# The adaLN condition of a hybrid layer: scale and shift summed on VectorE from the unsplit weights, the first norm applied by feature to the turned x, the gate's weights later in the plan

## What is computed

```
mod = silu(c) @ w_ada + b_ada                  # c: 1024 numbers, w_ada: 1024 x 3072
shift, scale, gate = split(mod, 3)             # 1024 numbers each
h = rms_norm(x, norm_g) * (1 + scale) + shift  # x: 256 x 1024
proj = h @ w_in                                # the four branches' q, k, v, z
...                                            # branches d, c, b, a, merged with sigmoid gates
x = x + gate * (merged @ w_out)
```

## Time and profile before

| | us |
|---|---|
| median of 3 runs | 1190.98 (1190.47 to 1192.14) |
| the profiled execution, its own time | 1190.06 |
| its span | 1188.8 |
| TensorE busy (matmul) | 1153.0 |
| VectorE, ScalarE, GpSimd busy | 735.2, 595.9, 48.3 |
| TensorE's clock granted, mean | 0.989 |

### The profile page before, as it was taken

One profiled execution on the slowest core, in us unless ns is written; L12 is line 12 of the kernel. 1 busy time (PEld: TensorE's weight loads), 2 busy tenths in 40 slices (PEclk: granted clock), 3 DMA queues, 4 the chain that ended last, 5 costly groups with the idle time before them and its releaser, 6 DMA issues.

```text
span 1188.8 us, 16723 instructions
## 1 busy us (share of the span) xinstructions
PE 1153.0 (97%) x7018; PEld 1024.4 (86%) x7018; DVE 735.2 (62%) x936; ACT 595.9 (50%) x824; POOL 48.3 (4%) x80
## 2 busy tenths in 40 slices
PE   6999999999999998999999999999899999999997
PEld 4799888788889987898999988787888989999985
DVE  5944766566677997755556655455767546555643
ACT  5545764344455662654545444445574555443431
POOL 3020100000000000000100000000003000000000
PEclk9999999899999999999999999999899999999999
DMA  9874543265546403543645545554326534546450
GB/s 352 300 246 117 184 137 130 89 230 183 206 146 212 161 1 107 177 141 107 166 159 200 188 164 193 189 187 155 101 93 196 178 106 163 180 172 207 137 188 36
DMA packets 105932, 195.70 MB, mean 165 GB/s; under 512 B 6033, under 2 KB 22561, under 8 KB 105856
## 3 DMA queue, kind: packets, MB, share of 16 engines
q1 hardware_dynamic: 102976, 186.46, 46.5%
q0 software_dynamic: 2880, 8.17, 2.4%
HBM read 193.56 MB, written 1.05 MB: 164 GB/s over the span
## 4 chain that ended last, share of the span: by engine, by line
PE 77%; DVE 12%; ACT 6%; issue 2%; DMA 1%; POOL 1%; SPq 0%; DVEq 0%; ACTq 0%; POOLq 0%
PE product L541 70%; DVE conv_out L2321 4%; ACT w_high L488 3%; DVE w_low L497 3%; DMA w_raw<-in_w_ada 1%; PE small L659 1%; PE small L1795 1%; PE small L1178 1%; ACT drows L2674 1%; PE small L574 1%; PE small L1189 1%; DVE drows L2750 1%; DVE stats L2752 1%; PE small L1816 1%; DVE drows L2765 0%
## 5 line engine op out<-in xcount | busy, mean ns | idle before, releaser
L497 DVE TENSOR_TENSOR w_low<-w_raw,w_high 128x2048 fp32r<-128x2048 f32 (+3 forms) x184 | 404.6, 2204 | 268.3 <-ACT w_high L488 264.5
L488 ACT ACTIVATE w_high<-w_raw 128x2048 fp32r<-128x2048 f32 (+3 forms) x184 | 338.0, 1841 | 180.3 <-PE product L541 161.9
L541 PE MATMUL product<-H_low,w_high 128*128 128x256 f32 x1080 | 307.6, 285 | 2.3 <-DVE w_low L497 1.3
L541 PE MATMUL product<-H_high,w_low 128*128 128x256 f32 x1080 | 305.9, 283 | 0.0
L541 PE MATMUL product<-H_high,w_high 128*128 128x256 f32 x1080 | 305.6, 283 | 0.0
L541 PEld LDWEIGHTS product<-H_low,w_high 128*128 128x128 f32 x1080 | 207.2, 192 | 4.5 <-issue 2.3
L541 PEld LDWEIGHTS product<-H_high,w_low 128*128 128x128 f32 x1080 | 207.2, 192 | 0.3
L541 PEld LDWEIGHTS product<-H_high,w_high 128*128 128x128 f32 x1080 | 207.2, 192 | 0.0
L541 PE MATMUL product<-w_high,H_low 128*128 128x512 f32 (+2 forms) x384 | 150.9, 393 | 0.0
L541 PE MATMUL product<-w_low,H_high 128*128 128x512 f32 (+2 forms) x384 | 149.0, 388 | 0.0
L541 PE MATMUL product<-w_high,H_high 128*128 128x512 f32 (+2 forms) x384 | 148.6, 387 | 0.0
(11 more groups left out here) (370 smaller groups left out, 1528.5 us busy)
## 6 DMA issues: line engine op xcount, KB each, us to landing
w_raw<-in_ffn_w_gate SPq DMA_DIRECT2D x20, 1024.0 KB, 5.1
w_raw<-in_ffn_w_up SPq DMA_DIRECT2D x20, 1024.0 KB, 5.2
w_raw<-in_ffn_w_down SPq DMA_DIRECT2D x20, 1024.0 KB, 5.1
w_raw<-in_w_merge SPq DMA_DIRECT2D x16, 1024.0 KB, 5.0
w_raw<-in_w_ada SPq DMA_DIRECT2D x12, 1024.0 KB, 6.5
w_raw<-in_w_in SPq DMA_DIRECT2D x8, 1024.0 KB, 5.2
w_raw<-in_mem_w_k SPq DMA_DIRECT2D x8, 1024.0 KB, 5.1
w_raw<-in_conv_w_pw SPq DMA_DIRECT2D x16, 512.0 KB, 4.4
```

Of the source, the lines that this page charges most:

```text
L488: k.act.eng.activation(chunk_view(k, k.w_high[j], i), chunk_view(k, k.w_raw[i % k.N_RAW], i), ACT.Copy).then_inc(*k.act.tells("weights_hig ...
L497: k.vec.eng.tensor_tensor(low, raw, high.bitcast(F32), ALU.subtract).then_inc(*k.vec.tells("weights_low", ("weights low", i)))
L541: mm = pe.eng.matmul(bank[:, off:off + wide], a, r, start=b not in started, stop=True, skip_group_check=True)
```

## The change

The weights of scale, shift and gate are no longer split and multiplied on TensorE. `vec_modulation` adds them up on VectorE from the raw buffer, a partition at a time: four operations of 128x512 per chunk, each weight row times its number of silu(c). What is left, a sum over the 128 partitions, is done on TensorE: for scale and shift by 4 matmuls per half with one column of ones (`pe_columns_of`), which puts feature by partition; for the gate by two matmuls with 128x128 ones (`mem()`), which spreads it over all partitions. x is turned first, only scaled by its root, and the norm is applied by feature by ScalarE (`act_first_half`), with low part on VectorE (`vec_first_low`). The plan moves the gate's four chunks between those of `w_in`, and the second half of shift behind the first chunk of `w_in`. x comes on SyncE's queue behind the first two chunks, and `norm_g` as 8 rows of 128.

```
+    first_in, shift = chunks(w_in, KT, [(W_D_Q, 512)]), modulation(ada, "shift", 1)
+    plan.extend(modulation(ada, "scale", 0) + modulation(ada, "shift", 0) + modulation(ada, "scale", 1) + first_in[:1] + shift + first_in[1:])
+    gate = modulation(ada, "gate", 0) + modulation(ada, "gate", 1)
+    for block in ((W_D_V, 512), (W_C_Q, 512), (W_C_V, 512)):
+        plan.append(gate.pop(0))
+        add(w_in, [block])
+    plan.append(gate.pop(0))
...
+def vec_split(k, n):
...
+        if i + 1 < len(k.plan) and k.plan[i + 1][2] and k.plan[i + 1][2][0] == "gate":
+            vec_modulation(k, *k.plan[i + 1][2])
+
+def vec_modulation(k, name, n, first):
+    V, i = k.vec, k.whole_weights[name, n, first]
+    raw, total = chunk_view(k, k.w_raw[i % k.N_RAW], i), k.sums_of[name][:, n * CN:(n + 1) * CN]
+    V.wait_ge("c silu", ("weights", i), "gate bias" if name == "gate" else None)
+    for j in range(CK):
+        number = k.c_silu[:, first + j:first + j + 1]
+        V.wait_ge(V.last)
+        if first + j == 0 and name != "gate":
+            V.eng.tensor_scalar(total, raw[:, j, :], number, None, ALU.mult).then_inc(*V.tells("modulations"))
+        else:
+            V.eng.scalar_tensor_tensor(total, raw[:, j, :], number, total, ALU.mult, ALU.add).then_inc(
+                *V.tells("modulations", (name, n), ("weights low", i)))
...
 def pe_condition(k):
...
+    tr(k.small.take("condition")[:, 0:3 * KT], k.cond_rows[:, :], k.ident[0:3 * KT, 0:3 * KT]).then_inc(*pe.tells("turned", "condition turned"))
+    pe_columns_of(k, "scale", 0)
+    pe_columns_of(k, "shift", 0)
+    for n in range(2):
+        pe_turn_x(k, n)
+    pe_columns_of(k, "scale", 1)
...
+def act_first_half(k, n):
+    A, columns = k.act, k.stat(("columns", n), 2 * CK)
+    for b in range(2):
+        for j in range(2):
+            f = 2 * b + j
+            A.wait_ge(("x turned", n, b), ("columns copied", n), ("whole free", n))
+            A.eng.activation(k.whole[:, f, :], k.small.of(("x", n, b))[:, S * j:S * (j + 1)], ACT.Identity, scale=columns[:, f:f + 1],
+                             bias=columns[:, CK + f:CK + f + 1]).then_inc(*A.tells("whole", k.small.free(("x", n, b))))
+        at = slice(CK * n + 2 * b, CK * n + 2 * b + 2)
+        A.wait_ge(A.last)
+        A.eng.activation(k.H_first.high[:, at, :], k.whole[:, 2 * b:2 * b + 2, :], ACT.Copy).then_inc(*A.tells("operand_high", ("first high", n, b)))
...
 def vec_condition(k):
     V = k.vec
+    V.mark(("whole free", 0))
+    for name in ("scale", "shift"):
+        for first in range(0, KT, CK):
+            vec_modulation(k, name, 0, first)
+    V.wait_ge("condition turned")
+    V.eng.tensor_copy(k.cond_cols[:, :], k.small.of("condition")[:, 0:3 * KT]).then_inc(*V.tells("cond_cols", k.small.free("condition")))
+    vec_modulation(k, "scale", 1, 0)
+    vec_first_columns(k, 0)
+    vec_modulation(k, "scale", 1, CK)
+    vec_first_low(k, 0)
     vec_split(k, 0)
+    for first in range(0, KT, CK):
+        vec_modulation(k, "shift", 1, first)
+    vec_first_columns(k, 1)
+    vec_first_low(k, 1)
     vec_split(k, 1)
...
 def pe_branches(k):
-        yield from pe_block(k, "d_qk", k.H_first, KT, FEATURES)
+        yield from pe_block(k, "d_qk", k.H_first, KT, FEATURES, inside={(0, 28): lambda: pe_columns_of(k, "shift", 1)})
...
     def mem():
+        for n in range(D // CN):
+            bank = k.small.take(("gate sums", n))
+            k.pe.wait_ge(("gate", n), k.small.before(("gate sums", n)))
+            k.pe.eng.matmul(bank[:, :], k.ones, k.gate[:, n * CN:(n + 1) * CN], start=True, stop=True).then_inc(*k.pe.tells("spread", ("gate sums", n)))
+        yield
```

More of the change, by code:

```diff
@@ L731, in vec_add @@
     add.then_inc(*V.tells("x_sums", ("x", norm.name, n, t), k.product.free(bank)))
-MODS = [("scale", 0), ("shift", 0), ("scale", 1), ("shift", 1), ("gate", 0), ("gate", 1)]
+ROWS = {"norm_g": 0, "shift": KT, "scale": 2 * KT}
 def pool_condition(k):
     w, g = k.w, k.pool
[L742 to L745, removed]
+    for name, vector in (("norm_g", w["norm_g"][0]), ("shift", w["b_ada"][0, 0:D]), ("scale", w["b_ada"][0, D:2 * D])):
+        g.eng.dma_start(k.cond_rows[ROWS[name]:ROWS[name] + KT, :], vector.rearrange("(k p) -> k p", p=P)).then_inc(*k.landed("load_rows", "condition rows"))
+    g.eng.memset(k.gate[:, :], 0.0).then_inc(*g.tells("pool_steps"))
+    g.wait_ge(g.last)
+    g.eng.dma_start(k.gate[0:1, :], w["b_ada"][0:1, 2 * D:3 * D]).then_inc(*k.landed("load_gate_bias", "gate bias"))
+    pool_inverse_root(k, "first", k.stat(("sums", "first"), NT), D, RMS_EPS, "first squares")
     at = 0
@@ L750, in pool_condition, with pe_columns_of @@
         at += n
-    pool_inverse_root(k, "first", k.stat(("sums", "first"), NT), D, RMS_EPS, "first squares")
     g.ended("condition")
     g.wait_ge(*k.all_ended("condition"))
+def pe_columns_of(k, name, n):
+    key, at = ("columns", n), CK * ("scale", "shift").index(name)
+    bank = k.product.take(key)
+    k.pe.wait_ge((name, n), "common", None if at else k.product.before(key))
+    for j in range(CK):
+        c = (CK * n + j) * P
+        mm = k.pe.eng.matmul(bank[:, at + j:at + j + 1], k.sums_of[name][:, c:c + P], k.ones[:, 0:1], start=at + j == 0, stop=True, skip_group_check=True)
+    mm.then_inc(*k.pe.tells("columns", key))
@@ L758, in pe_condition @@
     pe.wait_ge("common", "c row")
[L759 to L771, removed]
@@ L779, in act_condition @@
+    for t in range(NT):
+        A.wait_ge(A.last, ("root", "first"))
+        A.eng.activation(k.scaled_x[:, t, :], k.X[:, t, :], ACT.Copy, scale=k.stat(("root", "first"), NT)[:, t:t + 1]).then_inc(*A.tells("scaled_x", "scaled x"))
+    act_first_half(k, 0)
     act_split(k, 0)
+    act_first_half(k, 1)
     act_split(k, 1)
[L781 to L791, removed]
@@ L1522, in act_branches @@
     A, told = k.act, dict.fromkeys("abcd", 0)
-    A.wait_ge(("turned", ("first", 1, NT - 1)))
     def b_qk():
@@ L1589, in mem @@
     def mem():
+        for n in range(D // CN):
+            V.wait_ge(("gate sums", n))
+            V.eng.tensor_scalar(k.gate[:, n * CN:(n + 1) * CN], k.small.of(("gate sums", n))[:, :], 0.25, None, ALU.mult).then_inc(
+                *V.tells("gate", "layer gate", k.small.free(("gate sums", n))))
+        yield
         for t in range(NT):
```

116 lines of the change are left out of this document (60 added, 56 removed).

## The result

The changed kernel took 1180.68 us (1178.38 to 1181.28, 4 runs), the old one beside it 1190.72: 10.0 us less by the medians. The profiled execution took 1181.18 (span 1179.9). The forecast was 1180.0.

What follows compares the result with a forecast made beforehand. TensorE was taken to bound the kernel, behind a front until 57.25 us. `d_vz` 13.1 us earlier, less 2.1 for the gate's matmuls, gave 11.0: 1190.06 to 1179.06, plus 0.92 for the median: 1180.0 us, range 1175.5 to 1187.5.

Steps and rivals of the forecast that it cites:

- The front: All before TensorE's steady product, formerly until 57.25 us; its shortening was to bring `d_vz` 13.1 us earlier.
- step 0: TensorE's first part of `d_qk`, broken by a wait for shift's columns; start forecast at 32.0 us.
- step 1: TensorE's second part of `d_qk`, after some 5.6 us idle; start forecast at 47.15 us.
- the columns: Eight one-column matmul instructions on TensorE for shift's second half, inside step 0; forecast at 1.15 us.
- L: Landing of shift's first chunk, the third landing, from which the front's places are counted; forecast at 14.9 us.
- the first landing: First weight chunk arriving in SBUF; taken at 6.8 us as before, with later ones 2.7 us apart.
- The clock: After TensorE's idle 5.6 us, step 1 runs 5.3 us at half pace, costing 2.65 us; `d_vz` 0.9 us later.
- The gate: VectorE's last three gate chunks, 3.16 us each, cost nothing; TensorE's two gate matmuls add 2.1 us.
- Uncovered gate sums in the branches: Rival: gate sums on the path; all three 1189.5 us, one or two 1183 to 1186; 10%.
- A clock that stays low to the end of `d_vz`: Rival: TensorE stays at 1.2 GHz through `d_vz`, 1194.3 us, slower than before; 4%.
- A front held up by x or by slow transfers: Rival: x's load delays VectorE or transfers bind the first pass; at 300 GB/s 1184 us; 6%.
- The unforeseen gain: Rival that it goes better: splits overlap more than the rows bound, below 1175.5 us; 6%.

Runs made afterwards that it cites:

- e1_early: Changed kernel with both splits of the second `w_in` chunk ahead of the second half's norm; ratio 0.9866 to the old kernel.
- e7_early_gate_later: Changed kernel with the second `w_in` chunk split ahead of the second half's norm and gate chunks one place later; ratio 0.9863 to the old kernel.
- e3_gate_later_warm: Changed kernel with gate chunks one place later and eleven unused matmuls in TensorE's pause before step 1; 1178.55 us, ratio 0.9887 to the old kernel.
- e4_no_gate: Changed kernel without the gate's sums, eight columns copied and spread instead, chunks still loaded; ratio 0.9876 to the old kernel.
- e6_x_gpsimd: Changed kernel with x's load moved from SyncE's queue to GpSimd's, behind the three small rows; ratio 0.991 to the old kernel.
- e0_after: The changed kernel run again unchanged, on another chip; ratio 0.9899 to the old kernel.
- e8_shift_first: Changed kernel with all of shift ahead of `w_in`, both first `w_in` chunks split early on ScalarE, gate chunks later; ratio 0.9861 to the old kernel.
- e2_gate_later: Changed kernel with each gate chunk behind the first chunk of the following `w_in` block instead of ahead; 1179.03 us, ratio 0.9893 to the old kernel.
- e9_all: As e7_early_gate_later, plus four unused matmuls in TensorE's pause before step 1; ratio 0.9855 to the old kernel.
- e5_extra_op: Changed kernel with one more VectorE operation at the end of each of the twelve sum chunks; ratio 0.9939 to the old kernel.
- e10_rows_wait: Changed kernel with GpSimd's small loads waiting for the constants again, as before the change; ratio 0.9902 to the old kernel.

## Why the prediction was right, step by step

**The front.** The forecast put step 0 at 32.0, the last sum of shift at 38.05, step 1 at 47.15 and `d_vz` at 55.45. Measured were 33.65, 39.76, 48.95 and 57.05. Of each difference 1.65 us lies ahead of the whole chain: shift's first chunk landed at 16.54, not 14.9. From that landing on, step 0 came 17.1 us later, as forecast to a tenth, and `d_vz` 40.5 us later, as forecast too. The single terms: sum step 0.79 (0.79), the columns 1.07 (1.15), ScalarE's half norm 41.51 to 44.67, 3.2 (3.1), VectorE's wait for ScalarE 0.75 (0.45). That `d_vz` fits so closely is luck in part: step 1 started 0.15 us later after L than forecast and was 0.2 us shorter (8.10 instead of 8.3).

**The late landing is the term that was mis-sized.** The forecast took the first landing of the old trace, 6.8 us. In the twelve traces of the new kernel and its variants it came between 6.88 (e1_early) and 8.95 (e7_early_gate_later), in the old kernel at 6.84 and 7.00. The rest of the train held its spacing: L came 7.9 to 8.2 us behind the first landing wherever a wait shows it (forecast 8.1). The transfers themselves were hardly late. The window of the first 8 us in the new kernel, where the first chunk landed at 8.57, and then in e1_early, where it landed at 6.88:

```profile
0.00:8.00 8.00, 0.27 (x1) 0.18 (x1) 0.00 (x0) 1.46 (x2) 3.46 (x9) 1.00 0.72 248
```

```profile
0.00:8.00 8.00, 0.27 (x1) 0.18 (x1) 1.08 (x2) 1.46 (x2) 3.47 (x9) 1.00 0.76 264
```

At 248 GB/s 2.0 MB had moved by 8 us, with a first chunk of 1 MB not yet complete, against 2.1 MB in e1_early. That difference is worth 0.3 us at 390 GB/s, not 1.7. Why the first chunk is complete so late is open; the small loads' place and x's queue did not change it.

**The clock.** The choice between 5.3 us at half pace and none was right: 5.07 us (48.95 to about 54) at a granted clock of 0.50, the matmuls 0.22 us apart and not 0.24 as the forecast had it. The Trainium skill ("TensorE: Matmul & The Clock Gate", "The HAM clock gate (the "warmup" mystery)") says that idleness brings the half rate back; after the pause of 5.57 us this trace agrees, 0.50 in step 1. Step 1 took 8.10 us, 2.3 more than the 5.84 of e3_gate_later_warm (forecast 2.65); in all seven traces with a pause of 4.1 to 5.6 us before step 1 it was 1.7 to 2.6 more. In this kernel only 0.5 us of it counts (forecast 0.9), since the third low part was not there before 56.6 anyway (54.33 and half of 4.50, in VectorE's timeline).

**The gate.** That the sums of the last three chunks are hidden was right: VectorE busy 18.39 of 23 us, no new wait of TensorE. The first chunk stood ahead of the third low part, as forecast, and was covered by the slow step 1 alone: `d_vz` came no earlier in e4_no_gate, but in e1_early it waited for that low part. Its two matmuls took 1.72 us on the chain, not 2.1:

```profile
272.64 1.72 PE small L1574 x4
```

**The rivals.** Uncovered gate sums in the branches fall by the same rows. A clock that stays low to the end of `d_vz` falls by the window 54:57, 0.98. A front held up by x or by slow transfers falls by e6_x_gpsimd and by the spacing behind the first landing, though that landing was late. The unforeseen gain is not in this kernel: it took the order of e1_early.

**Why the total fits though the front gave less than forecast.** By `d_vz` the new trace leads by 68.80 - 57.05 = 11.75 us, not 13.1, and at the end of the span by 8.9, not 11. Between the two the gate's matmuls take 1.7 of it; the rest comes and goes with the clock in stretches that both kernels share. Between matching matmuls the lead is 11.8 us at 110 us of the old trace and 9.9 at 345, 1.8 apart; the forecast had named 2.1. In between it went up and down again. At about 205 us the old kernel ran slowly, without a wait:

```profile
205.00:207.00 2.00, 2.00 (x7) 1.78 (x8) 0.57 (x4) 0.34 (x2) 0.00 (x0) 0.50 0.50 189
```

The new one's clock fell at that place too, but later in it (0.76 at 193 to 195 us, 0.50 at 195 to 197), and it gained 1.6 us there. It lost 1.6 us at 227 (24 matmuls of L573 in 7.28 us; 5.67 before), and another 1.7 after the pause of 3.27 us at 442 (of it 1.3 in twelve matmuls that took 4.16 us; 2.86 in the earlier trace rows):

```profile
445.24 4.16 PE L2270 MATMUL small<-conv_out,mean_of 128*128 128x256 f32 x12 [3.27 <-DVE conv_out L2403]
445.00:449.00 4.00, 3.76 (x13) 3.16 (x13) 3.58 (x3) 0.00 (x0) 0.00 (x0) 0.70 0.14 15
```

So the steps do not sum to the span as forecast: it shrank by 8.9 us in these two executions, not 11. That the median is only 0.7 us from the forecast is luck in part, since it rests on where the clock fell in each execution and on the landing; with e0_after's 12.6 us the forecast of 11 lies between the two measurements.

## What to carry to other kernels

Forecast a front from its landing, with the price of each dependent operation, and then give the landing its own spread: here the chain behind it was right to 0.1 us and the landing itself off by 1.65. Judge an early first step by when the steady product starts, since e8_shift_first began 5 us later than e7_early_gate_later and reached `d_vz` 1.3 us behind it. Where two engines hand halves to each other, put the work that has its inputs (here the second split) in the idle time of the one that waits: this one move gave 3.6 us, the gate's place alone 0.4 (e2_gate_later, within the noise). At `d_vz` the two together gave more than their sum, 5.6 us after L against 3.8 and 0.6, but in part because the clock did not fall in e7_early_gate_later.

## What the hardware showed that I had not expected

**The same pause, another clock.** After 2.3 us without work TensorE's granted clock fell in e1_early and did not in e7_early_gate_later. The convolution has a pause of 3.27 us in every trace. From its last matmuls before that pause to the matmuls of the variance took 22.5 us in both traces of the old kernel, e0_after, e7_early_gate_later and e9_all, 24.1 to 24.2 in the new kernel's first trace, e3, e4, e5, e6 and e10, and 25.3 to 25.4 in e1, e2 and e8. This row of e1_early shows the worst, against 2.86 us in e0_after:

```profile
438.34 5.49 PE L2271 MATMUL small<-conv_out,mean_of 128*128 128x256 f32 x12 [3.26 <-DVE conv_out L2404]
```

e0_after and the new kernel's first trace are of the same program. So 1.5 to 3 us of a single trace of this kernel are chance at such places, as much as the smaller edits tried here; e9_all, with the lowest ratio, lost 3 us against e7_early_gate_later in its profiled execution between 200 and 240 us, at a granted clock of 0.87 (0.96 there).

**The clock also fell behind waits of about 1 us.** At the columns inside step 0 TensorE waited 0.85 us in e4_no_gate, 0.92 in e10_rows_wait and 1.52 in e5_extra_op, and soon behind it some 15 matmuls ran 0.21 us apart at a granted clock of 0.50. After 1.07 us in the new kernel, 1.08 in e0_after and 1.31 in e9_all they ran 0.12 us apart. Why is open. It cost nothing, since the pause before step 1 became 4.08 us instead of 5.57. The window behind the columns of e4_no_gate:

```profile
40.00:43.00 3.00, 3.00 (x16) 3.00 (x16) 0.92 (x3) 2.58 (x6) 0.00 (x0) 0.50 0.94 319
```

**The clock falls without any wait.** From 201 to 211 us the old kernel's TensorE was busy all the time, at first with 32 matmul instructions of 16 columns; the granted clock was 1.00 up to 203 us, 0.80 up to 205 and 0.50 from there to 211.

**Two groups of runs.** e8_shift_first's five runs lie at 1172.2 and 1172.3, and at 1177.6 to 1178.5, with nothing between. The mean granted clock was 0.991 in the first two and 0.981 to 0.987 in the other three, so the clock goes with it; where it fell is not known, as only one (1177.6) was profiled.
